# Attention rounds with the bias added by TensorE, exponentials and divisions one place earlier, and alternating low and high products in the GEMM

## What is computed

```python
s = jnp.einsum('bhqd,bhkd->bhqk', qb, kf).astype(jnp.float32) * scale + bias
return jax.nn.softmax(jnp.where(causal, s, -jnp.inf), axis=-1)
```

## Time and profile before

| | us |
|---|---|
| median of three runs | 1813.73 |
| profiled execution | 1813.74 |
| its span, first to last instruction | 1811.9 |
| PE busy | 1679.6 (93%) |
| PE weight loads busy (beside PE) | 1503.3 (83%) |
| DVE busy | 1259.5 (70%) |
| ACT busy | 943.6 (52%) |
| mean granted clock of PE | 0.970 |

### The profile page before, as it was taken

How to read it: one execution, slowest core, us unless ns; L and a number is a source line. 1 busy time by engine, 2 the same in 40 slices (tenths; PEclk the granted TensorE clock), 3 DMA queues, 4 the chain that set the end, 5 groups by cost and what they waited for, 6 DMA issues and landing times.

```text
span 1811.9 us, 28948 instructions
## 1 busy us (share of the span) xinstructions
PE 1679.6 (93%) x10664; PEld 1503.3 (83%) x10664; DVE 1259.5 (70%) x2043; ACT 943.6 (52%) x1634; POOL 14.2 (1%) x20
## 2 busy tenths in 40 slices
PE   6999999899999999996799999878999999779997
PEld 5888897798888888875788889767999788579986
DVE  6666766577776777766677776766877566577765
ACT  5555453555555555554465554355665443366652
...
GB/s 273 163 185 153 195 199 122 75 178 205 179 157 219 189 185 144 213 149 19 76 208 185 168 180 230 93 19 167 179 182 148 201 192 100 41 140 186 171 160 87
DMA packets 47360, 286.12 MB, mean 158 GB/s; under 512 B 5996, under 2 KB 6764, under 8 KB 23968
## 3 DMA queue, kind: packets, MB, share of 16 engines
...
q0 software_dynamic: 384, 0.68, 0.1%
HBM read 283.74 MB, written 1.05 MB: 157 GB/s over the span
## 4 chain that ended last, share of the span: by engine, by line
PE 84%; DVE 9%; ACT 5%; issue 2%; DMA 0%; ACTq 0%; DVEq 0%
PE ps_gemm L129 32%; PE ps_gemm L135 30%; PE ps_gemm L136 15%; DVE s_wlo L89 3%; ACT s_whi L80 1%; ACT s_work L819 1%; PE ps_gemm L808 1%; PE ps_sum L188 1%; PE ps_gemm L783 1%; DVE s_small L859 1%; DVE s_work L855 1%; PE ps_sum L808 1%; ACT s_work L828 1%; DVE s_work L878 0%; PE ps_sum L740 0%
## 5 line engine op out<-in xcount | busy, mean ns | idle before, releaser
L89 DVE TENSOR_TENSOR s_wlo<-s_wraw,s_whi 128x1024 fp32r<-128x1024 f32 (+3 forms) x608 | 630.2, 1078 | 413.8 <-ACT s_whi L80 413.7
L80 ACT ACTIVATE s_whi<-s_wraw 128x1024 fp32r<-128x1024 f32 (+3 forms) x608 | 539.6, 935 | 417.3 <-PE ps_gemm L136 209.5
L135 PE MATMUL ps_gemm<-s_xr,s_whi 128*128 128x512 f32 x1408 | 495.7, 397 | 5.4 <-DVE s_mem_v L694 3.1
L129 PE MATMUL ps_gemm<-s_xr,s_whi 128*128 128x256 f32 x2192 | 406.4, 288 | 10.3 <-DVE s_xr L249 7.9
L136 PE MATMUL ps_gemm<-s_xr,s_wlo 128*128 128x256 f32 x1408 | 394.4, 280 | 0.0
L135 PE MATMUL ps_gemm<-hid_r,s_whi 128*128 128x512 f32 x1056 | 370.9, 394 | 2.9 <-DVE hid_r L449 2.9
L129 PEld LDWEIGHTS ps_gemm<-s_xr,s_whi 128*128 128x128 f32 x2192 | 347.6, 195 | 16.0 <-issue 10.8
L135 PEld LDWEIGHTS ps_gemm<-s_xr,s_whi 128*128 128x128 f32 x1408 | 264.8, 188 | 69.8 <-issue 6.0
L129 PE MATMUL ps_gemm<-s_xr,s_wlo 128*128 128x256 f32 x1096 | 312.6, 285 | 0.0
L136 PE MATMUL ps_gemm<-hid_r,s_wlo 128*128 128x256 f32 x1056 | 294.7, 279 | 0.0
L136 PEld LDWEIGHTS ps_gemm<-s_xr,s_wlo 128*128 128x128 f32 x1408 | 266.3, 189 | 0.1
...
## 6 DMA issues: line engine op xcount, KB each, us to landing
...
```

The costliest lines, as they stand in the source:

```text
L80: c.act.activation(c.whi[:, slot, s], c.wraw[:, raw, s], ACT.Copy).then_inc(c.hi_ready, 1)
L89: last = c.dve.tensor_tensor(c.wlo[:, slot, s], c.wraw[:, raw, s], c.whi[:, slot, s].bitcast(F32), ALU.subtract)
L129: last = pe.matmul(out, a, b, start=start and i == 0, stop=stop and i == 2, skip_group_check=skip)
L135: pe.matmul(bank.rearrange("p (a t) -> p a t", t=T), w_hi, x_both, start=start, stop=False)
```

## The change

`mm_wide` takes the K step and its count in place of start and stop, and swaps its two products in odd steps. The bias of a job is no longer added by DVE: PE multiplies an identity with the bias table into the bank ahead of the scores, in fp32r (rounded twins of identity and tables, made by ACT at a new place each in mix_b and mix_e, semaphore `rounded`) or, in mix_o, in plain fp32. The tables of distances are multiplied by 8 on the host to stand ahead of the scale. DVE's pass L853/L855 is gone with its semaphore `scores_taken`; the reduce reads PSUM, the exponentials read PSUM with the scale, and a score bank is free once the exponentials are done (`exp_ready`). The exponentials, no longer the maxima, wait for the values of job n-3. In the rounds, ACT issues exponentials(i+2) ahead of outputs(i), and DVE divide(i+1) ahead of maxima(i+3), with maxima(2) ahead of the loop. In mix_a PE's weight unit 1 moves ahead of the scores of the second memory job. PE's wait for the tables of mix_o replaces DVE's. The callers of `exps_act` pass the bank; mix_b, mix_e and mix_o wait on `exp_ready` wherever they waited on `scores_taken`.

```diff
@@ -130,10 +130,14 @@
     return last
 
 
-def mm_wide(pe, bank, w_hi, w_lo, x_both, x_hi, start, stop):
-
-    pe.matmul(bank.rearrange("p (a t) -> p a t", t=T), w_hi, x_both, start=start, stop=False)
-    return pe.matmul(bank[:, 0:T], w_lo, x_hi, start=False, stop=stop)
+def mm_wide(pe, bank, w_hi, w_lo, x_both, x_hi, k, ks):
+
+    both, left = bank.rearrange("p (a t) -> p a t", t=T), bank[:, 0:T]
+    if k % 2 == 0:
+        pe.matmul(both, w_hi, x_both, start=k == 0, stop=False)
+        return pe.matmul(left, w_lo, x_hi, start=False, stop=k == ks - 1)
+    pe.matmul(left, w_lo, x_hi, start=False, stop=False)
+    return pe.matmul(both, w_hi, x_both, start=False, stop=k == ks - 1)
 
 
 def block(c, u, b):
...
@@ -774,15 +778,19 @@
     return c.ss[:, slot, 2 * h * job.width + k * P:2 * h * job.width + (k + 1) * P]
 
 
-def scores_pe(c, job, n, bank, part=None):
-
-    half = -(-len(job.scores) // 2)
-    maps = job.scores if part is None else job.scores[:half] if part == 0 else job.scores[half:]
-    for first, width, pairs in maps:
+def scores_pe(c, job, n, bank):
+
+    for first, ident, bias in job.bias:
+        cols = bias.shape[1] if len(bias.shape) == 2 else bias.shape[1] * bias.shape[2]
+        out = bank[:, first:first + cols]
+        if len(bias.shape) == 3:
+            out = out.rearrange("p (h w) -> p h w", w=bias.shape[2])
+        c.pe.matmul(out, ident, bias, start=True, stop=False, skip_group_check=True)
+    for first, width, pairs in job.scores:
         for a, (q, k) in enumerate(pairs):
-            last = c.pe.matmul(bank[:, first:first + width], q, k, start=a == 0, stop=a == len(pairs) - 1)
-    if part != 0:
-        last.then_inc(c.scores_ready, 1)
+            last = c.pe.matmul(bank[:, first:first + width], q, k, start=a == 0 and not job.bias, stop=a == len(pairs) - 1,
+                               skip_group_check=bool(job.bias))
+    last.then_inc(c.scores_ready, 1)
...
 
 
-def exps_act(c, job, n):
+def exps_act(c, job, n, bank):
     c.act.wait_ge(c.max_ready, n + 1)
-    s = n % 3
+    if n >= 3:
+        c.act.wait_ge(c.values_done, n - 2)
+    s, w = n % 3, job.width
     if job.sink is not None:
         c.act.activation(c.small[:, s, 48:48 + job.heads], c.small[:, s, 48:48 + job.heads], ACT.Exp)
     for h in range(job.heads):
-        e = c.ss[:, s, h * job.width:(h + 1) * job.width]
-        last = c.act.activation(e, e, ACT.Exp, bias=c.small[:, s, 16 + h:17 + h], accum_out=c.small[:, s, 32 + h:33 + h])
+        last = c.act.activation(c.ss[:, s, h * w:(h + 1) * w], bank[:, h * w:(h + 1) * w], ACT.Exp, scale=job.scale,
+                                bias=c.small[:, s, 16 + h:17 + h], accum_out=c.small[:, s, 32 + h:33 + h])
     last.then_inc(c.exp_ready, 1)
...
@@ -842,25 +852,27 @@
 
 def maxima_dve(c, cnt, job, n, bank):
 
-    dve, s, h, w = c.dve, n % 3, job.heads, job.width
+    dve, s, h = c.dve, n % 3, job.heads
     dve.wait_ge(c.scores_ready, n + 1)
-    if n >= 3:
-        dve.wait_ge(c.values_done, n - 2)
-    v = c.ss[:, s, 0:job.cols]
-    v3 = v.rearrange("p (h w) -> p h w", w=w)
-    src = bank[:, 0:job.cols]
-    if job.bias is None:
-        ins = dve.tensor_scalar(v, src, job.scale, None, ALU.mult)
-    else:
-        ins = dve.scalar_tensor_tensor(v3, src.rearrange("p (h w) -> p h w", w=w), job.scale, job.bias, ALU.mult, ALU.add)
-    ins.then_inc(c.scores_taken, 1)
-    dve.wait_ge(c.scores_taken, n + 1)
     m, nm, sd = (c.small[:, s, a:a + h] for a in (0, 16, 48))
-    dve_step(c, cnt, dve.tensor_reduce(m, v3, AX, ALU.max))
-    if job.sink is not None:
-        dve_step(c, cnt, dve.tensor_tensor(m, m, job.sink, ALU.max))
-        dve_step(c, cnt, dve.tensor_tensor(sd, job.sink, m, ALU.subtract))
+    dve_step(c, cnt, dve.tensor_reduce(m, bank[:, 0:job.cols].rearrange("p (h w) -> p h w", w=job.width), AX, ALU.max))
+    if job.sink is None:
+        dve.tensor_scalar(nm, m, -job.scale, None, ALU.mult).then_inc(c.max_ready, 1)
+        return
+    dve_step(c, cnt, dve.scalar_tensor_tensor(m, m, job.scale, job.sink, ALU.mult, ALU.max))
+    dve_step(c, cnt, dve.tensor_tensor(sd, job.sink, m, ALU.subtract))
     dve.tensor_scalar(nm, m, -1.0, None, ALU.mult).then_inc(c.max_ready, 1)
+
+
+def rounded_act_copy(c, twin, v):
+
+    c.act.activation(twin, v, ACT.Copy).then_inc(c.rounded, 1)
+
+
+def banked_bias(c, view, heads, w):
+
+    per = BANK // w
+    return [(i * BANK, c.ident_r[:, :], view(i * per, per)) for i in range(heads // per)]
...
@@ -910,7 +922,7 @@
     if cnt.out:
         pe.wait_ge(c.bank_free, cnt.out)
     if cnt.job:
-        pe.wait_ge(c.scores_taken, cnt.job)
+        pe.wait_ge(c.exp_ready, cnt.job)
     for i in range(2):
         scores_pe(c, jobs[i], cnt.job + i, c.score_banks[(cnt.job + i) % 2])
...
 
     pe = c.pe
-    pe.wait_ge(c.scores_taken, cnt.job + 1)
+    pe.wait_ge(c.exp_ready, cnt.job + 1)
     scores_pe(c, jobs[2], cnt.job + 2, c.score_banks[cnt.job % 2])
     for i, job in enumerate(jobs):
         n = cnt.job + i
         for g in range(job.groups):
             turn_pe(c, cnt, job, n, g, True)
         if i + 3 < len(jobs):
-            pe.wait_ge(c.scores_taken, n + 2)
+            pe.wait_ge(c.exp_ready, n + 2)
             scores_pe(c, jobs[i + 3], n + 3, c.score_banks[(n + 1) % 2])
         if n:
...
@@ -937,15 +949,15 @@
 
 
 def attention_act(c, cnt, jobs, after=None):
-    exps_act(c, jobs[0], cnt.job)
-    exps_act(c, jobs[1], cnt.job + 1)
+    for i in range(2):
+        exps_act(c, jobs[i], cnt.job + i, c.score_banks[(cnt.job + i) % 2])
     for i, job in enumerate(jobs):
         n = cnt.job + i
         for g in range(job.groups):
             turned_act(c, cnt, job, n, g, True)
+        if i + 2 < len(jobs):
+            exps_act(c, jobs[i + 2], n + 2, c.score_banks[n % 2])
         outputs_act(c, cnt, job, n, c.ps_gemm[:, 0, :])
-        if i + 2 < len(jobs):
-            exps_act(c, jobs[i + 2], n + 2)
         if after is not None:
             after(i)
...
@@ -955,12 +967,13 @@
     for i in range(2):
         maxima_dve(c, cnt, jobs[i], cnt.job + i, c.score_banks[(cnt.job + i) % 2])
     divide_dve(c, cnt, jobs[0], cnt.job)
+    maxima_dve(c, cnt, jobs[2], cnt.job + 2, c.score_banks[cnt.job % 2])
     for i, job in enumerate(jobs):
         n = cnt.job + i
-        if i + 2 < len(jobs):
-            maxima_dve(c, cnt, jobs[i + 2], n + 2, c.score_banks[n % 2])
         if i + 1 < len(jobs):
             divide_dve(c, cnt, jobs[i + 1], n + 1)
+        if i + 3 < len(jobs):
+            maxima_dve(c, cnt, jobs[i + 3], n + 3, c.score_banks[(n + 1) % 2])
         outputs_dve(c, cnt, job, n, c.ps_gemm[:, 0, :])
         if after is not None:
...
     scores_pe(c, jobs[0], n, c.ps_s)
     unit(0)
-    pe.wait_ge(c.scores_taken, n + 1)
+    unit(1)
+    pe.wait_ge(c.exp_ready, n + 1)
     scores_pe(c, jobs[1], n + 1, c.ps_s)
-    unit(1)
     unit(2)
...
-    pe.wait_ge(c.scores_taken, n + 2)
+    pe.wait_ge(c.exp_ready, n + 2)
     for h in range(A_HEADS):
...
     act.activation(b.cos[:, :], b.half[:, :], ACT.Sin).then_inc(c.b_sines_ready, 1)
+    act.wait_ge(c.b_in, 16 * 5)
+    rounded_act_copy(c, c.ident_r[:, :], c.ident[:, :])
+    rounded_act_copy(c, b.mask_r, b.mask)
     logs_act(c)
-    exps_act(c, jobs[0], n)
+    exps_act(c, jobs[0], n, c.ps_s)
     split_for(split_hi, c, cnt, u0 + 4)
...
         w = P * (blk + 1)
         q = slice(blk * P, (blk + 1) * P)
         for h0 in range(0, 4, heads):
-            bias = e.alibi[:, 2 * h0:2 * (h0 + heads), T - w:T]
+            bias = banked_bias(c, lambda h, n: e.alibi_r.rearrange("p (h t) -> p h t", t=T)[:, 2 * h0 + h:2 * h0 + h + n, T - w:T], 2 * heads, w)
...
+    act.wait_ge(c.e_tables_in, 16 * 5)
+    rounded_act_copy(c, e.alibi_r, e.alibi.rearrange("p h t -> p (h t)"))
+    rounded_act_copy(c, e.mask_r, e.mask)
     split_for(split_hi, c, cnt, u0 + 4)
     latent_hi(2)
     split_below(split_hi, c, cnt, u0 + 10)
...
         for j0 in range(0, 4, heads):
-            bias = (o.bias1 if blk else o.bias0)[:, j0 * 3 * w:(j0 + heads) * 3 * w].rearrange("p (h w) -> p h w", w=3 * w)
+            table, b0 = o.bias1 if blk else o.bias0, j0 * 3 * w
+            bias = [(i, c.ident[:, :], table[:, b0 + i:b0 + min(i + BANK, 6 * P)]) for i in range(0, 6 * P, BANK)]
             scores = [(((j - j0) * 3 + g) * w, w, [(o.q[:, 2 * g + j // 2, q], o.k[:, 4 * g + j, 0:w])])
                       for j in range(j0, j0 + heads) for g in range(3)]
...
     jobs = dilated_jobs(c, o)
+    pe.wait_ge(c.o_tables_in, 32)
     first_scores_pe(c, cnt, jobs)
     attention_pe(c, cnt, jobs)
...
@@ -2155,7 +2183,6 @@
     dve_step(c, cnt, dve.tensor_tensor(a0[:, :, 0:P], a0[:, :, 0:P], strict, ALU.mult))
     dve.tensor_tensor(a1, a1, strict, ALU.mult).then_inc(c.o_probs_ready, 1)
     values(1)
-    dve.wait_ge(c.o_tables_in, 32)
...
     slopes = np.repeat(2.0 ** (-2.0 * np.arange(1, 5)), 2)[None, :, None]
```

(33 more changed lines are left out.)

23 lines of the change are left out of this document (14 added, 9 removed).

## The result

The changed kernel takes 1794.21 us in the median of five runs (1789.62 to 1801.50) against 1813.73 for the kernel before beside it. The ratio is 0.9906, 95% interval 0.9884 to 0.9928: 13 to 21 us less. A second series of six runs, beside eleven of the kernel before (1812.24), gave 1795.03 and 0.9915 (0.9894 to 0.9937). The profiled run is the fastest of its five, 1789.62 with a span of 1787.8, so its trace shows more gain, 24.1 us, than the medians.

A forecast was written before the change was run, and what follows sets the result against it. PE holds 84% of the chain, so gains must come from its waits in the attention rounds. Terms -10-2.5-2.9-1+0.1+0 sum to -16.3, from 1813.74 to 1797.4 us; range 1788 to 1808.

The forecast's parts named there:

- A: Whole kernel: the prediction's own sum of terms, 1797.4 us, own range 1792 to 1803; chance 0.56.
- Window rounds of mix_b: Six jobs of mix_b: first transposes +1.6 us, then 25.2 us to the projection, -10 (bounds -7 and -12).
- the weight split: Work of ACT and DVE in the first round of mix_b, of which 1.3 us was let show.
- mix_e: Rounds of mix_e: exponentials move ahead, -2.06 us, and 0.4 of two removed passes; -2.5 (0 to -4.2).
- that sign: In mix_e, values(3) would come without the 3 us of idle, if the prediction was right.
- mix_o: In mix_o: first transposes +1.1 us, three PE-bound rounds at 4.6, three at 3.0; -2.9 (+3 to -5).
- Memory jobs: In mix_b: the 1.22 us pass goes from in front of the first transposes; -1 us (-2 to +1).
- GEMM order: Wide GEMM product pairs, now 0.354 us each: alternation taken as 0, with -7.4 to +3.7 us, up to +6, weighed.
- The reduce from PSUM: DVE's reduce costed the same, 1.22 us a job; the Trainium skill's estimated 65 ns more left out of the sum.
- Rival D: Attention rounds: half the gain, exponentials of i+2 not ready and rounding behind them; 1803 to 1809 us, chance 0.14.
- Rival E: Attention rounds: slower because PE's idle before scores(2) of mix_b brings 1.2 GHz; up to 1838 us, chance 0.07.

The follow-up runs named there:

- E3: The kernel before with only the new orders of ACT and DVE, DVE's scale-and-bias pass kept: 1804.98 us, ratio 0.9955.
- E2: The kernel before with only the alternating product order of mm_wide, mixers unchanged: 1812.29 us against 1811.24, ratio 1.0005.
- E7: The changed kernel without PE's bias products, masks and biases left out of the softmax: one run, 6.3 us less in mix_o, rounds of mix_b 24.2 us.
- E1: The changed kernel with the old product order, high ahead of low in every K step: 1796.31 us, ratio 0.9911.
- E5: The changed kernel with only ACT's order undone, rounding ahead of exponentials: 1808.11 us, ratio 0.9969, rounds of mix_b 32.9 us.

## Why the prediction was right

Forecast 1797.4 us and -16.3; measured 1794.21, -17 by the ratio (13 to 21), -15.4 in the second series. The case was A, and the terms stand one by one:

- **Window rounds of mix_b**, forecast +1.6 for the start and 25.2 us of rounds, -10: +1.8 and +2.8 for the start, 23.9 us of rounds, and 1.5 given back because the projection starts at a low clock: -9.6 and -8.6. The rounds bound by PE took 4.4, 4.9, 4.3 where I had 5.7, 4.4, 4.4: the weight split showed in the second round, with 0.5 us of idle, not 1.3. The sum took full clock in the rounds without giving it a term; it held (0.99), and it is 5.3 us of the gain.
- **mix_e**, forecast -2.5: -1.5 and -1.6. values(3) still wait 2.15 us for ACT's copies, so that sign came only in part. In the chain of the changed kernel the head norm stands in front of them (square L726 0.61, then the copies L838 0.98); the exponentials are gone from it, as forecast.
- **mix_o**, forecast -2.9: -2.4. The first transposes come 1.2 us later, forecast 1.1; PE bound the rounds at 4.4, 4.5 and 4.8, forecast 4.6. E3 shows -3.2 there with the order alone, but E2 shows -1.8 with nothing changed there, so whether the new home of the bias costs anything net isn't settled. If it were free, mix_o would be 6.3 us shorter (E7). I had priced the fp32 bias rightly, at 1.3, and not asked what it kept the order from earning.
- **Memory jobs**, forecast -1: -2.8 and -2.9. E2, in which nothing of this is changed, has -1.5 in the same stretch from the clock alone, so the change has about -1.3.
- **GEMM order**, forecast 0: 0 (E1, E2). Of the two prices weighed, the rows held: 350.6 ns a pair on average. The 354 of the forecast was one stretch; the kernel before has 350.3 over its whole trace. The trace does not agree with the estimated 325 ns that the formula of the Trainium skill (TensorE: Matmul & The Clock Gate, "Back-to-back issue gap") makes; the page gives it for isolated matmuls.
- **The reduce from PSUM**, costed the same: L858 takes 1.22 us, from PSUM, as L859 did from SBUF. The estimated 65 ns more that the cycle table of the Trainium skill (VectorE: DVE Perf Modes, the section on the TRN2 errata) would make are not in the trace.

Rival D (half the gain) is nearest to E5 in time, 6 us of gain, but not in mechanism: there the exponentials stand behind the rounding, not the rounding behind them. In the changed kernel D doesn't happen: ACT's exponentials (L828) show no idle before them in any round of mix_b, so their maxima were ready. Rival E (the clock) showed its first step, the scores at 1.2 GHz behind 4.31 us of idle, and stopped there: mix_b went from 0.79 to 0.95, mix_o to 1.00.

What the prediction had wrong without showing in the sum is how the parts combine. Rival D named one such case, that only the removed passes count, and put it at half the gain; no sum was made for either part alone. Alone the order gives 5.5 us in mix_b's rounds and the removed pass 2.8; together 12.9. It also read that PE is the limit of none of the old rounds. In the first, 847.30 to 854.00, PE was busy for all of the 6.70 us, at a clock of 0.54.

That the total came so close is partly luck. The changed stages add up to -16.3 and -15.5 us in the two profiles, but E2 has -3.2 in the same stages with nothing changed in them, so they are not known to the microsecond. The first profile gained 7.8 us besides, in stretches to which the forecast gave nothing.

What the start to mix_b gained (-3.8, -3.7) isn't settled. E2 and E3, with the same code there apart from the products, have -2.3 and +2.7.
